# Fp32 transformer blocks on one core: weights as the stationary operand in three SwiGLU stages, and the eighth expert unrolled with filler products behind it

## The reference

```python
def modulated_residual(x, c, g, w_mod, b_mod, fn):
    shift, scale, gate = ada_params(c, w_mod, b_mod)
    h = rms_norm(x, g) * (1 + scale) + shift
    return x + gate * fn(h)

def swiglu(h, w_gate, w_up, w_down):
    return (jax.nn.silu(h @ w_gate) * (h @ w_up)) @ w_down

for e in range(N_EXPERTS):      # 8 experts, top 2 of each token
    out = out + gates[..., e:e + 1] * swiglu(h, w_gate[e], w_up[e], w_down[e])
```

## Time and profile before

| | |
|---|---|
| median of 3 runs | 1996.34 us |
| the profiled execution | 1994.08 us |
| its span | 1991.9 us |
| PE busy | 1876.0 us (94%) |
| DVE busy | 1635.4 us (82%) |
| ACT busy | 1136.0 us (57%) |
| moved by DMA | 551.08 MB, mean 277 GB/s |

### The profile page before, as it was taken

How to read it: one execution, slowest core, us unless ns; L and a number is a source line. 1 busy time by engine, 2 the same in 40 slices (tenths; PEclk the granted TensorE clock), 3 DMA queues, 4 the chain that set the end, 5 groups by cost and what they waited for, 6 DMA issues and landing times.

```text
span 1991.9 us, 29287 instructions
## 1 busy us (share of the span) xinstructions
PE 1876.0 (94%) x9218; PEld 1547.2 (78%) x9218; DVE 1635.4 (82%) x2193; ACT 1136.0 (57%) x1616; POOL 36.0 (2%) x47
## 2 busy tenths in 40 slices
PE   3999999988999999999999999978899999789998
PEld 2987887866788888888888888866678887667886
DVE  6999886768989898989898989897876759786554
ACT  2444444464777777777777777654544444554442
POOL 2000000000000000000000000000000000000000
PEclk9999999999999999999999999988999999899999
DMA  9978996557799999999999999958568875846762
GB/s 330 343 250 307 345 362 188 171 175 243 262 343 362 340 362 339 364 337 364 337 364 335 365 335 365 337 200 216 170 217 268 271 241 157 264 140 190 217 218 72
DMA packets 368474, 551.08 MB, mean 277 GB/s; under 512 B 35827, under 2 KB 293110, under 8 KB 368342
## 3 DMA queue, kind: packets, MB, share of 16 engines
q1 hardware_dynamic: 365392, 547.81, 82.2%
q10 hardware_dynamic: 2118, 1.46, 0.3%
q0 software_dynamic: 832, 0.30, 0.1%
HBM read 548.38 MB, written 1.08 MB: 276 GB/s over the span
## 4 chain that ended last, share of the span: by engine, by line
PE 84%; DVE 8%; ACT 3%; DMA 2%; issue 2%; POOL 0%; SPq 0%; DVEq 0%; ACTq 0%; POOLq 0%
PE ps L429 25%; PE ps L431 25%; PE ps L430 25%; ACT prob L1311 2%; PE ps L940 2%; PE ps L1116 2%; PE ps L991 2%; DMA mod_in<-in_w_mod 1%; DVE mod_acc L1634 1%; PE ps L925 1%; DVE x_tokens L1661 1%; DVE x_normed L1660 1%; DVE units_low L424 1%; PE ps L751 1%; PE ps L913 0%
## 5 line engine op out<-in xcount | busy, mean ns | idle before, releaser
L424 DVE TENSOR_TENSOR units_low<-raw_units,units_high 128x1024 fp32r<-128x1024 f32 (+1 forms) x838 | 980.5, 1218 | 96.0 <-ACT units_high L420 90.2
L420 ACT ACTIVATE units_high<-raw_units 128x1024 fp32r<-128x1024 f32 (+1 forms) x838 | 843.5, 1058 | 244.3 <-PE ps L431 209.5
L429 PE MATMUL ps<-units_high,hT_high 128*128 128x512 f32 (+1 forms) x1568 | 619.8, 395 | 8.3 <-DVE hT_low L1703 3.8
L431 PE MATMUL ps<-units_high,hT_low 128*128 128x512 f32 (+1 forms) x1568 | 615.2, 392 | 0.0
L430 PE MATMUL ps<-units_low,hT_high 128*128 128x512 f32 (+1 forms) x1568 | 610.9, 390 | 0.0
L429 PEld LDWEIGHTS ps<-units_high,hT_high 128*128 128x128 f32 x1568 | 295.7, 189 | 76.3 <-issue 8.3
L431 PEld LDWEIGHTS ps<-units_high,hT_low 128*128 128x128 f32 x1568 | 295.1, 188 | 65.6
L430 PEld LDWEIGHTS ps<-units_low,hT_high 128*128 128x128 f32 x1568 | 295.3, 188 | 63.7 <-issue 0.2
L429 PE MATMUL ps<-units_high,aT_high 128*128 128x512 f32 x632 | 258.8, 409 | 1.2 <-DVE qkT L1869 0.6
L431 PE MATMUL ps<-units_high,aT_low 128*128 128x512 f32 x632 | 248.2, 393 | 0.0
L430 PE MATMUL ps<-units_low,aT_high 128*128 128x512 f32 x632 | 246.5, 390 | 0.0
(11 more groups left out here) (279 smaller groups left out, 1373.7 us busy)
## 6 DMA issues: line engine op xcount, KB each, us to landing
raw_units<-in_moe_w_gate SPq DMA_DIRECT2D x352, 256.0 KB, 4.6
raw_units<-in_moe_w_up SPq DMA_DIRECT2D x352, 256.0 KB, 5.8
raw_units<-in_moe_w_down SPq DMA_DIRECT2D x176, 512.0 KB, 6.4
mod_in<-in_mod_w SPq DMA_DIRECT2D x96, 512.0 KB, 6.0
mod_in<-in_w_mod SPq DMA_DIRECT2D x96, 512.0 KB, 5.4
raw_units<-in_w_gu SPq DMA_DIRECT2D x176, 256.0 KB, 3.6
raw_units<-in_w_down SPq DMA_DIRECT2D x44, 512.0 KB, 4.3
raw_units<-in_w_in SPq DMA_DIRECT2D x32, 512.0 KB, 6.9
```

Of the source, the lines that this page charges most:

```text
L420: eng.activation(whi[:rows, high_slot(f, n), 0:width], raw[:rows, raw_slot(f, n), 0:width], ACT.Copy).then_inc(f.hi, 1)
L424: eng.tensor_tensor(low[:rows, raw_slot(f, n), 0:width], raw[:rows, raw_slot(f, n), 0:width], whi[:rows, high_slot(f, n), 0:width].bitcast ...
L429: pe.matmul(dst, ah, bh, start=start, stop=False, **kw)
L431: return pe.matmul(dst, al, bh, start=False, stop=stop, **kw)
```

## The change

It has two parts.

**Dense stages.** The three calls of `swiglu` with two tiles become calls of a new function `dense`. Gate and up have the weights stationary and `hT` moving (256 columns, all tokens), 24 matmuls a unit. The result lies in PSUM with the hidden columns on the partitions, which is the form that the down part needs, so there are no transposes. `act` goes straight to ACT (high part, read from SBUF) and DVE (low part). The down part of j-1 follows the gate and up of j. `sum_gate` stands ahead of the last down part. ACT and DVE split one unit between silu and the high part, and between the product and the low part.

**Experts.** The loop runs over experts 1 to 6; expert 7 is written out without the gather and its split. `BRIDGE` gets 34 filler matmuls of 512 columns before `normed_T(4)`.

```diff
+DENSE_LEAD = 5
...
+def dense_order():
+    order = []
+    for j in range(STEPS + 1):
+        if j < STEPS:
+            order += [("gu", j, u) for u in range(4)]
+        if j >= 1:
+            order += [("down", j - 1, u) for u in range(FK)]
+    return order
...
-BRIDGE = (0, 14, 0, 12, 0, 0, 0, 0)
+BRIDGE = (0, 14, 0, 12, 34, 0, 0, 0)
...
+    def dense_split_ahead(j):
+        return min(DENSE_POS["gu", j, 3] + 1 + DENSE_LEAD, FFN_UNITS) if j < STEPS else FFN_UNITS
...
+        def dense(f, n0, step0, gate):                       # PE
+            for j in range(STEPS + 1):
+                if j < STEPS:
+                    bank = 0 if j == 0 else 4
+                    if j > 1:
+                        pe.wait_ge(f.act, step0 + j)
+                    for u in range(4):
+                        n = n0 + DENSE_POS["gu", j, u]
+                        pe.wait_ge(f.lo, n + 1)
+                        for kk in range(2):
+                            k = 2 * u + kk
+                            if j == 0:
+                                pe.wait_ge(s_htl, first_ht + k + 1)
+                            for c in range(4):
+                                col = kk * 512 + c * P
+                                last = product(pe, ps[:, bank + c // 2, (c % 2) * S:(c % 2 + 1) * S],
+                                               whi[:, high_slot(f, n), col:col + P],
+                                               low[:, raw_slot(f, n), col:col + P],
+                                               hTh[:, k, :], hTl[:, k, :], start=k == 0 and c % 2 == 0,
+                                               stop=k == DC - 1, skip_group_check=True)
+                        last.then_inc(f.used, 1)
+                if j == STEPS:
+                    pe.wait_ge(f.act, step0 + STEPS)
+                    sum_gate(gate)
+                if j >= 1:
...
+                    pe.wait_ge(f.atl, step0 + i + 1)
...
-        swiglu(fa, N_FFN0, 0, T, gate=1)
+        dense(fa, N_FFN0, 0, 1)
...
+        def dense(f, n0, step0, skip, gate):                 # ACT
+            k = skip
+            for j in range(STEPS + 1):
+                while k < dense_split_ahead(j):
+                    split_high(ac, f, n0 + k)
+                    k += 1
+                if j < STEPS:
+                    bank = 0 if j == 0 else 4
+                    ac.wait_ge(f.used, n0 + DENSE_POS["gu", j, 3] + 1)
...
+                    ac.activation(gu_silu[:, :, :].rearrange("p a b -> p (a b)"), ps[:, bank, :], ACT.Silu)\
+                        .then_inc(f.silu, 1)
+                    if k < FFN_UNITS:
+                        split_high(ac, f, n0 + k)
+                        k += 1
+                    ac.wait_ge(f.act, step0 + j + 1)
+                    ac.activation(aTh[:, j % 2, :, :], act[:, :, :], ACT.Copy).then_inc(f.ath, 1)
+                else:
+                    mod_gate(gate)
...
+        def dense(f, n0, step0, skip, between):              # DVE
...
+                ve.wait_ge(f.silu, step0 + j + 1)
...
+                ve.tensor_tensor(act[:, :, :].rearrange("p a b -> p (a b)"),
+                                 gu_silu[:, :, :].rearrange("p a b -> p (a b)"), ps[:, bank, :], ALU.mult)\
+                    .then_inc(f.act, 1)
+                if k < FFN_UNITS:
+                    unit(k)
+                    k += 1
+                ve.wait_ge(f.ath, step0 + j + 1)
+                ve.tensor_tensor(aTl[:, j % 2, :, :], act[:, :, :], aTh[:, j % 2, :, :].bitcast(F32), ALU.subtract)\
+                    .then_inc(f.atl, 1)
...
-        def expert(it):
+        def expert(it, following=True):
...
+            hooks = {("after_T", 1): scat0, ("after_T", 2): scat1, ("after_T", 3): hot_T}
+            if following:
+                hooks["before_T", STEPS] = lambda: gather(it + 2)
...
-        with pe.Fori(1, E) as it:
+        with pe.Fori(1, E - 1) as it:
             expert(it)
+        expert(E - 1, following=False)
         with pe.If(more > 0):
+            gather(E + 1)
...
-        pe.wait_ge(s_xel, done + 2)
+        pe.wait_ge(s_xel, done + 1 + more)
```

More of the change, by code:

```diff
@@ L1205, in _ @@
             first_ht = HT(s + 1)
-            swiglu(fb, n0 + N_FFN2, l * STEPS, T, gate=s + 1)
+            dense(fb, n0 + N_FFN2, l * STEPS, s + 1)
     @block.scalar
@@ L2081, in _ @@
         expert(0)
-        with ve.Fori(1, E) as it:
+        with ve.Fori(1, E - 1) as it:
             expert(it)
+        expert(E - 1, following=False)
         with ve.If(more > 0):
+            xe_low(E + 1)
             with ve.Fori(E, 2 * E) as it:
```

101 lines of the change are left out of this document (76 added, 25 removed).

## The result

The changed kernel takes **1984.6 us** (median of 5 runs, 1983.4 to 1990.2) against 1996.3 us; the ratio to the kernel before is 0.9949 (95% interval 0.9935 to 0.9964), so 10.2 us less [7 to 13]. The forecast was 1980.3, 16.0 less. The sign was right; a third of the gain did not come. By the ratio (0.9949 times 1996.34 is 1986.2) the time lies just past the end of the range, 1986; the median of 1984.6 alone lies inside it. The profiled execution took 1983.38 us (1994.08 before), so its trace shows a difference of the same size.

What follows compares the result with a forecast made beforehand. PE was taken to bound the dense stages, DVE the stretches between. Dense stages 11.4, eighth expert 4.0 and clock 0.6 sum to 16.0 us less, taking the median from 1996.34 to 1980.3; range 1972 to 1986.

Steps and rivals of the forecast that it cites:

- the forecast 4.6: Behind the eighth expert: 4.0 us from `y_low` coming sooner without the gather, and 0.6 from PE's clock.
- Rival D: Behind the eighth expert: the gain does not come through because DVE's chain or the loads hold; 1985 us, chance 0.08.
- The 34 fillers: Behind the experts: 7.8 us of fillers in 8.63 us of PE idle time, ending 0.8 before the rows, delaying nothing.
- The clock's term: Behind the experts: fillers keep PE at 2.4 GHz, first products at full pace give 0.6 us; bounds 0 and 1.4.
- Dense stages: 11.4 forecast: Three dense stages: 7.4 - 3.8 - 1.5, 7.4 - 4.0 - 1.5 and 7.4, together 11.4 us less.
- transposes and pause: Each dense stage: 11 fewer groups of transposes save 5.1 us; the second step's wait, now covered, saves 1.1.
- G: End of a dense stage: the first matmul of `sum_gate`, from which later times are counted; 327.12 before.
- Its price of 1.5 each: Behind the first two dense stages: PE's clock falls to half in idle time, costing 1.5 us each; bounds 0 and 3.
- Rival A: Dense stages' gate and up: short matmuls carry long ones' fixed cost; 2012 us, or 2008 at 2.93 a unit; chance 0.06.
- its weaker form: Dense stages: about 2.5 ns per matmul beyond its columns, so the three lose 4.0 us, not gain 3.6; 1988 us.
- Rival B: Ends of dense stages are not delayed: 3.8 + 4.0 + 3.0 us come back, 1969.5 us; chance 0.12.
- Rival C: First dense stage: DVE becomes the bound, half a microsecond over on ten steps, 1985 us; chance 0.07.

Runs made afterwards that it cites:

- near path: Changed kernel, DVE's usual path laid right behind its test, second pass after it: 1978.5 us; same layout with only the experts' part on the kernel before: 0.9980.
- the dense stages alone: The kernel before with only the dense-stage part of the change; experts 1 to 7 all in the loop, no 34 fillers: 0.9945.

## Why the prediction was right and wrong, point by point

**What failed: "`weighed`, which I let begin at about 1290.4 (the last low part of `act` and the branch done)".** It began at 1294.82, in a loop that ran 0.95 us ahead. The prediction gives the branch no term of its own: from the end of the last low part (1292.70 - 3.57 = 1289.1) to 1290.4 it leaves 1.3 us for it. Before, the branch took 0.56 us; behind written-out code it took 6.9, so `y_low` came 0.5 us later than before and not 4.0 sooner.

The rest of the mechanism was right for DVE: with the near path `y_low` does come 4.05 us sooner on the kernel before. It left out PE, whose scattered rows then came only 2.1 sooner (1297.80 for 1299.89). So the 4.0 us of that run beside the forecast 4.6 is partly luck. In the change itself the 4.6 were taken back whole: 2.0 us more when this half stands alone, between 1.0 less and 4.8 more. The profile's "issue 2%" and the order of the code, a loop of some 190 DVE instructions between branch and target, were both before me.

The Trainium skill has the rule, in "Runtime: NRT & Kernel Launch", Instruction fetch mechanics: "A taken branch whose target isn't in the current 2-page window forces a DMA fetch of the target page before execution can continue". The trace agrees: 5.6 to 8.1 us in the six kernels with the far target behind straight code, 0.2 with a near one, 0.05 on the path that falls through. That before and the dense stages alone escape with 0.56 would fit if there the target happened to lie in the window; no run here shows the window. The same section of the Trainium skill says that kernels prefer full unrolling where possible for this reason; here one turn was written out and the branch stayed, and that made it late. What the experiments show is that the place of the code decides; that the time is spent in a fetch is the Trainium skill's account of it, and no run here shows it directly.

**Rival D** ("the experts' gain does not come through", 0.08, 1985) gave nearly the right time (1984.6, or 1986.2 by the ratio) and the right place for the wrong reason; its chance was too low, because only data was thought of as a cause.

**The 34 fillers**: forecast to end 0.8 us before the rows, they ended 1.2 behind them. They were counted against rows 4 us sooner but with a PE that would come with them; PE's sums started late and at half clock. The clock's term came through: the difference of +1.43 at the transposes is +0.52 at the first product behind them, 0.9 gained for a forecast of 0.6.

**Dense stages: 11.4 forecast, 11.0 measured.** The terms, one by one: transposes and pause as forecast. G came 1.87 us sooner in a stage at the fast pace (forecast 1.91), 0.93 where 118 ns held for the first 28 us; that was the mis-sized term, 2.72 us a unit with 2.96 as its bound. `residual` at G+7.08 (7.2). Idle 5.12 and 5.37 (5.3), half clock as forecast. Its price of 1.5 each was too high: with fillers at full clock 0.9 and 0.7 us were gained on the way and none was left at the mixer's end. The third stage gave its 5.5 at the end.

**Not foreseen**: the first dense stage's gain of 3.44 us at its end was 0.93 at the first gather, held up by a modulation block that landed late and by the transposes at half clock behind it (behind the second layer's mixer, above). From the first dense stage's start to the first gather 0.3 us were gained for a forecast of 2.1; from the second's to the third's 3.9 for 1.9. One part of that was luck: from 1706 to 1722 us the kernel before had a mean granted clock of 0.68, the changed one 0.89 in the same work (1702 to 1718). So the agreement of 11.4 and 11.0 is partly chance.

**Rival A** (short products carry the fixed cost of long ones) is true in a weaker form, in 3 stages of 30 throughout and in 7 for two steps: 2.83 us a unit, where it had 2.93. At 118 ns two short products cost 236 ns against 229 of a long one, at 113.3 they cost 227. So its weaker form in the prediction (4.0 us lost over the three stages, 1988) did not come at the faster pace, where short products gain 1.2 us a stage as forecast. Two levels were not among my cases; I had taken the convolution's 2.96 us for a start-up effect.

**Rival B** was wrong as a forecast: the ends were delayed. As an offer it was too large: it had 10.8 us coming back, and reordering DVE's queue brings 3.8, since later waits take a part of what the transposes gain. **Rival C**: DVE was no bound, each step took 16.40 us.

## What to carry to other kernels

Idle time with no releaser behind a branch was late code here. Where you see it, lay the path that is usually taken right behind the test, on every engine that has the branch, and read the trace again, since the latest engine hides the next one's lateness. A loop unrolled for its last turn moves the branch to straight code; count that as a risk of several us. When work is taken from the bound engine near a stage's end, ask which queue order was free only because that work covered it.

## What the runs showed of the hardware that was not expected

- A taken branch to code some 190 instructions ahead took DVE 5.6 to 8.1 us when it came from straight code, while DMA moved 349 GB/s (1288.5 to 1294.7 us in the changed kernel), and 0.56 us when it came from the loop. PE stood 2.8 us without a releaser at its own branch, behind nine products, and not at all once its usual path was laid right behind the test.
- Back-to-back products of 256 columns have two paces, 113.3 and 118 ns, at a granted clock of 1.00 throughout. With nothing inserted a stage is in one from its first product, and either keeps the slower one or leaves it after two steps. One product of 16 columns turned the step behind it slower in three stages of three; ten, one in each step but the first, turned all the steps behind them. Products of 512 columns hardly show it (176.8 us a stage, to 0.03, nine times).
- Run to run the first kernels with short products scatter more than the kernel before (1992.8 to 1998.9 in 17 runs): the dense stages alone 1982.0 to 1994.5 us, where the profiled execution is the 1994.5, with two stages at 179.6. The later ones, whose stages all take 174.95 us in the traces, do not: the near path has 1976.7 to 1982.4.
